# A two-layer hybrid decoder step: all adds of the normed sums to x on VectorE

## What is computed

```
def _rms_norm(x, w):
    xf = x.astype(jnp.float32)
    y = xf * lax.rsqrt(jnp.mean(xf * xf, axis=-1, keepdims=True) + RMS_EPS)
    return (y * w.astype(jnp.float32)).astype(x.dtype)
...
    for i in range(DEPTH):
        h = _rms_norm(x, W['norm_mix_pre'][i])
        mix, pool_new, C_new, n_new, m_new, gv_rows = _mixer(h, i, W, pool_prev[i], C0[i], n0[i], m0[i], start_pos)
        x = x + _rms_norm(mix, W['norm_mix_post'][i])
        h = _rms_norm(x, W['norm_ffn_pre'][i])
...
        x = x + _rms_norm(f, W['norm_ffn_post'][i])
        gate = jax.nn.sigmoid(_rms_norm(x, W['norm_ple'][i]) @ W['ple_w_gate'][i])
        x = x + gate * (p[i].astype(x.dtype) @ W['ple_w_proj'][i])
```

## Time and profile before

| what | value |
|---|---|
| median of 3 runs | 1739.98 us (1739.64 to 1748.13) |
| the profiled execution | 1741.73 us, span 1740.0 us |
| TensorE busy | 1677.7 us (96%) |
| VectorE busy | 686.1 us (39%) |
| ScalarE busy | 562.8 us (32%) |
| GpSimd busy | 253.8 us (15%), of which 27.0 us in the adds |
| stretches of the normed sums | N = 0: 272 to 300 us; N = 1: 673 to 708; N = 2: 1007 to 1029; N = 3: 1671 to 1695 |

### The profile page before, as it was taken

The page is one execution under the profiler, slowest core; times in us unless marked ns, Lnnn a source line. Parts: engine busy times, 40 slices in busy tenths (PEclk is TensorE's granted clock), DMA queues, the critical chain, the costliest instruction groups (busy, mean ns, idle before and its releaser), DMA issues.

```text
span 1740.0 us, 29427 instructions
## 1 busy us (share of the span) xinstructions
PE 1677.7 (96%) x12422; PEld 1543.7 (89%) x12422; DVE 686.1 (39%) x1034; ACT 562.8 (32%) x950; POOL 253.8 (15%) x323
## 2 busy tenths in 40 slices
PE   7999998999999998989999979999999999999988
PEld 6878898999999997988779968998988989889988
DVE  3444455444244434554434450324133142242355
ACT  5232444322122323442324451313133132231252
POOL 5643121000000001216421021000000000002010
PEclk9999999999999999999999986999999999999999
DMA  5345261223232321413352325787877877869312
GB/s 171 86 80 115 78 209 60 91 91 112 71 97 84 115 79 49 127 61 75 92 119 64 121 106 170 237 281 242 277 281 227 291 258 244 296 231 347 106 50 86
DMA packets 73062, 260.02 MB, mean 149 GB/s; under 512 B 10152, under 2 KB 10672, under 8 KB 72928
## 3 DMA queue, kind: packets, MB, share of 16 engines
q1 hardware_dynamic: 59760, 219.52, 38.5%
q0 software_dynamic: 13184, 38.79, 8.0%
HBM read 237.20 MB, written 21.31 MB: 149 GB/s over the span
## 4 chain that ended last, share of the span: by engine, by line
PE 91%; DVE 4%; ACT 2%; issue 1%; DMA 1%; DVEq 0%; ACTq 0%; SPq 0%; POOL 0%; POOLq 0%
PE lin L714 71%; PE aux L714 19%; DVE zreg L1755 1%; DVE h_lo L1758 1%; ACT h_hi L1245 1%; DMA region_y<-yslot,idxg 1%; PE aux L1009 1%; DVE zreg L1758 0%; DVE x L1755 0%; ACT htok L1245 0%; PE aux L1011 0%; ACT region_y L1245 0%; DMA wreg<-in_w_in_slabs 0%; DVE wlo L1755 0%; PE aux L859 0%
## 5 line engine op out<-in xcount | busy, mean ns | idle before, releaser
L714 PE MATMUL lin<-h_hi,whi 128*128 128x260 f32 x1616 | 432.6, 289 | 23.2 <-DVE h_lo L1758 23.2
L714 PE MATMUL lin<-h_lo,whi 128*128 128x260 f32 x1616 | 424.3, 284 | 0.0
L714 PEld LDWEIGHTS lin<-h_hi,whi 128*128 128x128 f32 x1616 | 307.9, 191 | 33.0 <-issue 27.3
L714 PE MATMUL lin<-h_hi,wlo 128*128 128x260 f32 x1616 | 327.5, 284 | 0.0
L714 PEld LDWEIGHTS lin<-h_lo,whi 128*128 128x128 f32 x1616 | 307.3, 190 | 0.6
L714 PE MATMUL lin<-zreg,wreg 128*128 128x160 f32 x2048 | 285.6, 301 | 1.7 <-issue 1.7
L714 PEld LDWEIGHTS lin<-zreg,wreg 128*128 128x128 f32 x2048 | 282.0, 192 | 5.0 <-issue 4.9
L714 PEld LDWEIGHTS lin<-h_hi,wlo 128*128 128x128 f32 x1616 | 251.4, 190 | 0.0
L1755 DVE TENSOR_TENSOR wlo<-wreg,whi 128x1024 fp32r<-128x1024 f32 (+1 forms) x140 | 180.6, 1291 | 88.4 <-ACT whi L1245 88.4
L1245 ACT ACTIVATE whi<-wreg 128x1024 fp32r<-128x1024 f32 (+1 forms) x140 | 152.0, 1089 | 71.1 <-DMA wreg<-in_ffn_w_down 26.9
L1755 DVE TENSOR_TENSOR region_b<-zreg,lin 128x160 f32<-128x160 f32 x88 | 28.3, 321 | 322.0 <-PE lin L714 322.0
(11 more groups left out here) (325 smaller groups left out, 2449.9 us busy)
## 6 DMA issues: line engine op xcount, KB each, us to landing
wreg<-in_moe_w_gate SPq DMA_DIRECT2D x64, 512.0 KB, 5.2
wreg<-in_moe_w_up SPq DMA_DIRECT2D x64, 512.0 KB, 6.0
wreg<-in_moe_w_down SPq DMA_DIRECT2D x56, 512.0 KB, 4.5
wreg<-in_w_in_slabs SPq DMA_DIRECT2D x44, 512.0 KB, 3.6
ring_more<-in_moe_w_gate SPq DMA_DIRECT2D x24, 512.0 KB, 4.5
ring_more<-in_moe_w_up SPq DMA_DIRECT2D x24, 512.0 KB, 4.4
wreg<-in_ffn_w_gate SPq DMA_DIRECT2D x22, 512.0 KB, 3.5
wreg<-in_ffn_w_up SPq DMA_DIRECT2D x22, 512.0 KB, 3.5
```

The source lines that it names most:

```text
L714: return nc.tensor.matmul(out, lhsT, rhs, start=start, stop=stop)
```

## The change

GpSimd's `add_x` and its two calls go, and `x_pool` with them. VectorE adds every chunk, one pass behind its product: in pass c it adds chunk c - 1, for c from 1 to 8, from the `ut` buffer of that chunk's parity. `x_dve` now counts all chunks in order, and ScalarE and TensorE wait for that count alone.

```diff
-            def add_x(N):
-
-                for c in range(1, DC, 2):
-                    pool.wait_ge(ut_ready, N * DC + c + 1)
-                    pool.tensor_tensor(x[:, c], x[:, c], ut[:, 1], ALU.add).then_inc(x_pool, 1)
...
-                add_x(2 * L)
...
-                add_x(2 * L + 1)
...
                     for c in range(DC):
-                        pe.wait_ge((x_dve, x_pool)[c % 2], DC * L + c // 2 + 1)
+                        pe.wait_ge(x_dve, 2 * L * DC + c + 1)
...
                 def wait(c):
-                    act.wait_ge((x_dve, x_pool)[c % 2], N * DC // 2 + c // 2 + 1)
+                    act.wait_ge(x_dve, N * DC + c + 1)
...
                     if c < DC:
                         if N or c >= 2:
-                            dve.wait_ge((x_dve, x_pool)[c % 2], N * DC // 2 + c // 2)
+                            dve.wait_ge(x_dve, N * DC + c - 1)
                         stt(ut[:, c % 2], acc[:, c], cols[:, w + c:w + c + 1], rn, ALU.mult, ALU.mult).then_inc(ut_ready, 1)
-                    if c % 2 and c < DC:
+                    if 1 <= c <= DC:
                         dve.wait_ge(ut_ready, N * DC + c)
-                        tt(x[:, c - 1], x[:, c - 1], ut[:, 0], ALU.add).then_inc(x_dve, 1)
+                        tt(x[:, c - 1], x[:, c - 1], ut[:, (c - 1) % 2], ALU.add).then_inc(x_dve, 1)
```

More of the change, by code:

```diff
@@ L333, in build @@
         h_hi_ok, h_ready, h_free = sem("h_hi_ok"), sem("h_ready"), sem("h_free")
-        ut_ready, x_dve, x_pool, ple_x = sem("ut_ready"), sem("x_dve"), sem("x_pool"), sem("ple_x")
+        ut_ready, x_dve, ple_x = sem("ut_ready"), sem("x_dve"), sem("ple_x")
         gw_in, gw_ok, gw_lo = sem("gw_in"), sem("gw_ok"), sem("gw_lo")
```

## The result

| | before | changed kernel |
|---|---|---|
| median | 1742.18 us (22 runs, 1735.25 to 1748.13) | 1745.88 us (22 runs, 1742.22 to 1747.54) |
| profiled execution | 1741.73 us, span 1740.0 | 1745.92 us, span 1744.1 |

The ratio is 1.002, 95% interval 1.0012 to 1.0027: some 3.5 us slower (0.002 x 1742), clear of noise but well inside 0.5%. With more runs beside it the kernel before has a median 2.2 us above the one of its first three.

What follows compares the result with a forecast made beforehand. TensorE, busy 1677.7 of 1740.0 us, was taken as the bound. Terms 1.0 + 1.5 - 1.4 + 4.0 = +5.1 us on the three-run median 1739.98 gave 1745.1 us, range 1739.8 to 1750.0.

Steps and rivals of the forecast that it cites:

- The period: VectorE's chain of add, ScalarE's rounding, low part and product was to take 2.83 us per chunk.
- N = 3: Normed sum of layer 1 after the experts: TensorE waits for each chunk, +4.0 us, all on the path.
- L(0): VectorE's low part of x, chunk number in brackets; in N = 3 chunk 0's was to start at 1675.21.
- N = 1: Normed sum of layer 0 after the FFN: early shift kept through the projections, then a longer end, +1.5 us.
- N = 0: Normed sum of layer 0 after the mixer: TensorE's queue hides most of the longer chain, +1.0 us.
- N = 2: Normed sum of layer 1 after the mixer, squares summed, no low part: VectorE's stalls go, -1.4 us.
- The layer-1 loads: Loads GpSimd issued after the adds of N = 1 no longer stand behind them; given nothing.
- All that follows hangs on these means: Root, routing and ScalarE's scaled rows behind TensorE's means of N = 2 were to follow them; no further difference forecast.
- A: Rival: the low part keeps its 0.84 us, period 2.99 us, sum +7.7, 1747.7 us; chance 0.14.
- B: Rival: stalls beside GpSimd's adds in N = 2 come off in full, -4.2 us; total 1739.8 us; chance 0.12.
- C: Rival: TensorE's clock falls in N = 3, gate slabs behind lose 8.5 us; total 1753.6 us; chance 0.11.
- D: Rival: N = 3 is hidden too because ScalarE answers faster, +1.1, 1741.1 us; chance 0.03 with the rest.

Runs made afterwards that it cites:

- e1: Changed kernel with the low part moved behind product and add in each pass: 1735.48 us, ratio 0.9961 to the kernel before.
- e2: Changed kernel with the add put ahead of the product, low part still first: 1737.82 us, ratio 0.997 to the kernel before.
- e3: Kernel before with the change in N = 2 alone, GpSimd's adds kept in the other three sums: 1738.77 us, ratio 0.9979.
- e6: Changed kernel with the order add, low part, product in each pass: 1736.48 us, ratio 0.9971 to the kernel before.
- e4: Kernel before with the change in N = 0, N = 1 and N = 3, GpSimd's adds kept in N = 2: 1747.5 us, ratio 1.003.
- e5: Changed kernel plus four GpSimd adds in N = 2 on unrelated tiles that nobody needs: 1749.38 us, ratio 1.0048 to the kernel before.

## Why the prediction was right

**The period.** 2.83 us per chunk was forecast from three pieces of the trace before (add to low part 1.48, low part to product 0.68, product to add 0.67); it is 2.84, made of 1.50, 0.67 and 0.67 (1676.45, 1677.95, 1675.11, 1675.78). The rows of the kernel before gave a chain that it never ran as a whole; that worked because each piece was taken from start to start on the engine that carries the chain, ScalarE's share included. e1 shows from the other side that the chain is the cause: with the same instructions and no wait the period is 1.95.

**N = 3.** L(0) came 0.10 us earlier than forecast and L(7) at 1694.31 (forecast 1694.35). The step to the path was also right: TensorE took the last chunk 0.06 us after the low part ended, and +4.18 us stayed.

**N = 1.** The first product came 1.37 us later than before; with that taken off, L(1) starts at 680.24 (forecast 680.23) and L(7) at 703.98 (703.99). The round through p keeps the shift, as forecast.

**N = 0.** The view shows the two waits as 0.26 us and not 0.45 to 0.5, but TensorE's steps there are 2.84 us apart (292.64 to 295.48) for 2.31 before, 0.53 us per chunk, and the term is +1.15 for +1.0. Its mechanism, a queue that lasts four chunks, holds.

**N = 2.** With the shift of 3.02 us in the first product taken off, the means start at 1023.70 (forecast 1023.65). Of the 4.2 us of removed stalls (0.92 and three times 1.10) the four adds that VectorE makes now take back 2.4 (0.61 each); TensorE, last as forecast, takes another 0.4, and 1.35 is left.

**The layer-1 loads** that no longer stand behind GpSimd's adds were put at nothing: from N = 1 to N = 2 it is 304.03 us before and 304.08 after.

**The step that failed** is "All that follows hangs on these means", with no difference behind it, and with it the premise that only a wait or an earlier start of TensorE moves the end: from N = 2's means to N = 3 the changed kernel is 1.79 us shorter, because TensorE's clock differs at two places. The stretch at the lower of its two levels (granted clock 0.50, 1.2 GHz), of which the prediction showed the piece from 1039 to 1056, runs from about 1031 to 1072 in both kernels. The view by windows, before:

```profile
1031.00:1072.00 41.00, 34.22 (x112) 28.81 (x113) 6.64 (x40) 10.86 (x14) 10.86 (x12) 0.51 0.33 121
...
1616.00:1618.00 2.00, 1.94 (x9) 1.97 (x10) 1.09 (x1) 0.00 (x0) 0.00 (x0) 0.50 0.64 262
```

And after (first the window, then its length, the busy time of PE, PEld, DVE, ACT and POOL, the granted clock, DMA share and GB/s):

```profile
1031.00:1072.00 41.00, 34.17 (x121) 27.78 (x121) 7.55 (x49) 10.55 (x13) 10.88 (x12) 0.51 0.33 121
...
1617.00:1619.00 2.00, 1.74 (x15) 1.77 (x16) 1.30 (x2) 0.00 (x0) 0.00 (x0) 1.00 0.75 307
...
1672.00:1697.00 25.00, 19.73 (x127) 17.47 (x127) 16.43 (x24) 12.96 (x22) 0.00 (x0) 1.00 0.15 43
1697.00:1742.00 45.00, 41.11 (x340) 40.78 (x339) 22.96 (x30) 13.51 (x18) 0.00 (x0) 1.00 0.27 89
```

The work lies 1.67 us later in it (the means at 1026.72 for 1025.05), so the stretch takes in more of the routing, where TensorE often waits, and less of the expert's matmuls behind it, where it does not. The two chains of work, before and then after, show what comes of that, with the second place further down:

```profile
1066.66 51.09 PE lin L714 x352
...
1616.06 1.94 PE aux L1051 x8
1618.00 4.90 PE lin L714 x32
```

```profile
1068.99 49.79 PE lin L706 x352
...
1617.26 1.06 PE aux L1043 x8
1618.33 4.35 PE lin L706 x32
```

The same 352 matmuls take 1.30 us less; 0.66 of it went into the routing (they start 42.27 us after the means instead of 41.61), 0.65 us is left. That much goes with N = 2: in the five profiles with its adds on VectorE and nothing on GpSimd (the changed kernel, e1, e2, e3, e6) the clock falls 5 us after the means, in the kernel before and e4 7 us after, and where the chain leaves the experts, before the last gather, the first five stand 573.64 to 573.73 us after the means, the other two 574.22 and 574.36. (In e5, with its means 4 us later, it falls 7.7 us after them.)

The other 1.1 us lies behind that gather. The profiled execution before has a short low stretch at 1616, that of the changed kernel has none: the 8 and 32 matmuls there take 5.41 us for 6.84, and some 0.3 of the difference is lost again on the way to N = 3. Of the other profiles e1, e2 and e4 have a low stretch there, e3, e5 and e6 none; one profile of each kernel does not say whether the change has a part in it. The mean granted clock of many executions says more: it is 0.978 in the 26 and 17 executions of the kernel before that ran beside the experiments, 0.980 in the 22 of the changed kernel, and 0.979 to 0.981 in those of each of e1 to e6, e4 among them. So on average every variant loses less to the clock than the kernel before, whether N = 2 was changed in it or not. An estimate, as if TensorE were on the path throughout: 0.0016 (a mean of 0.9798 for 0.9782) of 1740 us is 2.8 us, which takes the +5.6 us of the four terms to about +3, and 3.5 were measured. Why the clock does so stays open.

**The rivals.** A (a low part after a wait costs 0.84): no, 0.76 us after 0.80 us of waiting, in every row. It was the GpSimd add. B (the relief wins): its mechanism is shown by e5, its size was wrong, as in N = 2 VectorE's own adds and then TensorE took most of it. C (the clock falls in N = 3): no; it reads 1.00 from 1672 to 1697 and from 1697 to 1742 above, with TensorE busy for 19.73 of the first 25 us. The Trainium skill, page TensorE: Matmul & The Clock Gate, Part 1, section What's actually happening, makes the clock follow recent activity; here a microsecond of idling in every 2.84 did not bring it down. D: no; L(7) is as late as the chain says.

**The forecast time** of 1745.1 us meets the measured 1745.88 better than its parts do, and that is luck, as two errors cancel: the difference was 1.0 us too large by the spans (+5.1 for +4.1; 1.6 by the ratio), and the median it was added to, of three runs, 2.2 us low.

## What to carry to other kernels

When an engine takes over work that another did beside it, look at the order in its loop before its busy share: an instruction that waits for another engine's answer should stand as far as possible behind the one that sets that engine going. Here the same three instructions give periods of 2.84, 2.17, 2.08 or 1.95 us, by where they stand in the pass, and turn +0.2% into -0.4%. What counts is how many instructions lie between the add and the low part of the same chunk (none, one, three and three), not which comes first in the loop's text. Split a change that acts at several places and measure the parts (e3 and e4): a small total can be a gain and a loss.

## What the runs showed of the hardware

- An unrelated GpSimd add costs VectorE as much as a related one: a VectorE sum or product of two 128x520 float32 tensors takes 1.67 to 1.79 us instead of 0.69 to 0.76 and ends 0.55 us after the add.
- It works the other way too. The third add of e5 is recorded from 1022.17, yet the sum that VectorE starts at 1022.56 takes its usual 0.69 us and the add 2.22 us instead of 1.62: the later one went first. Its recorded start does not tell who does.
- The low stretch of TensorE's clock behind N = 2 (granted clock 0.50) lasts 41 us in both kernels, and two microseconds of its place against the work are worth 0.65 us. A short one behind the last gather stands in the profiles of the kernel before, e1, e2 and e4 and not in those of the changed kernel, e3, e5 and e6, and is worth about as much as a whole term of the sum.
- Executions of one kernel spread with the clock: the 26 of the kernel before beside e1 to e4 go from 1736.94 us at a mean granted clock of 0.979 to 1747.18 us at 0.975, almost three times the size of the change.
